# Weighted rows of the second experts added on TensorE at the end of a hybrid attention, HGRN2 and mixture-of-experts step

## What is computed

```python
x = x + concat([att, rec]) @ w_o
h = rmsnorm(x, norm2_g)
for e in range(N_EXPERTS):                      # each row: its two best experts
    y = (silu(h @ w_gate[e]) * (h @ w_up[e])) @ w_down[e]
    out = out + gates[..., e:e + 1] * y
x = x + out
y_prompt, y_sample = rmsnorm(x, final_norm_g)
```

## Time and profile before

| | |
|---|---|
| median of three runs | 523.42 us (521.96 to 525.18) |
| the profiled execution | 524.19 us |
| its span in the trace | 522.4 us |
| PE busy | 471.7 us (90%) |
| DVE (VectorE) busy | 336.5 us (64%) |
| ACT (ScalarE) busy | 232.0 us (44%) |
| POOL (GpSimd) busy | 105.7 us (20%) |
| DMA, mean over the span | 178 GB/s |

### The profile page before, as it was taken

The page is one execution under the profiler, slowest core; times in us unless marked ns, Lnnn a source line. Parts: engine busy times, 40 slices in busy tenths (PEclk is TensorE's granted clock), DMA queues, the critical chain, the costliest instruction groups (busy, mean ns, idle before and its releaser), DMA issues.

```text
span 522.4 us, 7082 instructions
## 1 busy us (share of the span) xinstructions
PE 471.7 (90%) x2493; PEld 371.8 (71%) x2493; DVE 336.5 (64%) x658; ACT 232.0 (44%) x448; POOL 105.7 (20%) x168
## 2 busy tenths in 40 slices
PE   6999899999999999999999887999999999999400
PEld 6879799877996777778877686676766776677100
DVE  4777515586585357766554689697478567765176
ACT  6664711563356447224121335466367356544021
POOL 5148001111000000001000143030322322312143
PEclk9999999999999999999999959899999999999855
DMA  8804404004008500510110878999899999800295
GB/s 306 194 6 163 169 0 162 0 1 162 1 1 218 163 11 4 178 41 0 41 60 3 304 271 344 421 404 373 333 367 377 375 342 358 338 23 27 69 332 189
DMA packets 33101, 93.16 MB, mean 178 GB/s; under 512 B 10248, under 2 KB 13456, under 8 KB 26928
## 3 DMA queue, kind: packets, MB, share of 16 engines
q1 hardware_dynamic: 27728, 82.81, 44.0%
q0 software_dynamic: 5344, 9.97, 5.4%
HBM read 88.38 MB, written 13.89 MB: 196 GB/s over the span
## 4 chain that ended last, share of the span: by engine, by line
PE 77%; DVE 11%; DMA 5%; ACT 4%; issue 1%; SPq 1%; POOL 0%; POOLq 0%; ACTq 0%; DVEq 0%
PE ps L2069 11%; PE ps L1745 7%; PE ps L1747 7%; PE ps L1746 7%; PE ps L2089 6%; PE ps L2091 5%; PE ps L2090 5%; PE ps L1957 3%; PE ps L1959 3%; PE ps L1958 3%; DMA pair<-y_pairs 2%; PE ps L2050 2%; PE ps L1982 1%; PE ps L1900 1%; PE ps L1897 1%
## 5 line engine op out<-in xcount | busy, mean ns | idle before, releaser
L1610 DVE TENSOR_TENSOR gu_lo<-we_gu,gu_hi 128x1024 fp32r<-128x1024 f32 x64 | 74.8, 1219 | 3.0 <-ACT gu_hi L1004 1.5
L1004 ACT ACTIVATE gu_hi<-we_gu 128x1024 fp32r<-128x1024 f32 x64 | 63.2, 1055 | 3.0 <-DMA we_gu<-in_w_up 3.0
L2069 PE MATMUL ps<-we_d,hhT 128*128 128x512 f32 x128 | 56.9, 592 | 0.0
L2089 PE MATMUL ps<-gu_hi,xT_hi 128*128 128x512 f32 x128 | 52.7, 411 | 2.6 <-DVE xT_lo L1604 2.5
L2091 PE MATMUL ps<-gu_hi,xT_lo 128*128 128x512 f32 x128 | 50.9, 397 | 0.0
L2090 PE MATMUL ps<-gu_lo,xT_hi 128*128 128x512 f32 x128 | 50.5, 395 | 0.0
L1745 PE MATMUL ps<-hT_hi,w_hi 128*128 128x288 f32 x160 | 48.5, 303 | 1.7 <-DVE w_lo_q L1103 0.8
L2069 PEld LDWEIGHTS ps<-we_d,hhT 128*128 128x128 f32 x128 | 23.4, 191 | 24.9 <-issue 24.9
L1745 PE MATMUL ps<-w_hi,hT_hi 128*128 128x512 f32 x96 | 39.1, 407 | 0.0
L1746 PE MATMUL ps<-w_lo,hT_hi 128*128 128x512 f32 x96 | 37.5, 391 | 0.0
L1745 PEld LDWEIGHTS ps<-hT_hi,w_hi 128*128 128x128 f32 x160 | 30.1, 188 | 5.0 <-issue 2.6
(11 more groups left out here) (394 smaller groups left out, 1122.3 us busy)
## 6 DMA issues: line engine op xcount, KB each, us to landing
we_gu<-in_w_gate SPq DMA_DIRECT2D x16, 1024.0 KB, 7.7
we_gu<-in_w_up SPq DMA_DIRECT2D x16, 1024.0 KB, 13.0
we_d<-in_w_down SPq DMA_DIRECT2D x16, 1024.0 KB, 12.3
ring<-in_w_in SPq DMA_DIRECT2D x4, 2048.0 KB, 7.7
pair<-y_pairs SPq DMA_DIRECT2D x8, 512.0 KB, 7.7
ring<-in_w_in SPq DMA_DIRECT2D x3, 1024.0 KB, 8.1
x_first<-in_x_p SPq DMA_DIRECT2D x4, 512.0 KB, 9.7
x<-in_x_p SPq DMA_DIRECT2D x4, 512.0 KB, 3.7
```

The lines of the kernel that those rows point to most:

```text
L1004: act.activation(gu_hi[slot % 2][:, :, 2 * q:2 * q + 2, :], we_gu[slot][:, :, 2 * q:2 * q + 2, :], ACT.Copy).then_inc(gu_hi_done, 1)
L1610: dve.tensor_tensor(gu_lo[slot][:, :, 2 * q:2 * q + 2, :], we_gu[slot][:, :, 2 * q:2 * q + 2, :], gu_hi[slot % 2][:, :, 2 * q:2 * q + 2, : ...
L2069: last = pe.matmul(bank(4 + 2 * (slot % 2) + half), hhT[:, slot % 2, f, :], we_d[slot][:, f, 512 * half:512 * half + 512], start=f == 0, s ...
L2089: pe.matmul(bank(0), xT_hi[:, c, :], gu_h[:, :, c, :], start=c == 0, stop=False)
```

## The change

For tiles 1 to 4 the residual and the second experts' rows are added on TensorE. Four diagonal 128x128 matrices with the second gates on their diagonals are made by VectorE at the end of `weights()`, in the memory of a gain that is no longer needed (`ng_bc`). After the last group of blocks TensorE multiplies the identity with x of tiles 1 to 4, each tile into two banks of PSUM, and then, when a tile's second rows have landed, adds the diagonal matrix times these rows in the same banks. VectorE's `weigh_first(t)` adds the first experts' rows, weighted, to what stands in PSUM and writes x. Tile 0 keeps its two instructions. The ten loads are issued in another order, and the finals of tiles 1 to 4 stand behind all of the weighing.

```diff
+        diag = ng_bc[:, :].rearrange("p (t k) -> p t k", t=NT - 1)
...
+        diag_ready, added = sem("diag_ready"), sem("added")
...
-            for t in range(NT):
-                for i in range(2):
+            for t, i in ((1, 1), (0, 0), (2, 1), (0, 1), (3, 1), (1, 0), (4, 1), (2, 0), (3, 0), (4, 0)):
                     cols = slice(i * D, (i + 1) * D)
                     sp.dma_start(pair[0:rows_of(t), t, cols], pairs[tok(t), cols]).then_inc(pair_in[i][t], 16)
...
-                act.wait_ge(sum_ready, 2 * t + 2)
+                act.wait_ge(sum_ready, t + 2)
...
                 dve.tensor_tensor(gates[:, 1, :], gates[:, 0, :], rb[:, :, 4], ALU.mult).then_inc(gates_ready, 1)
+                dve.wait_ge(gates_ready, 1)
+                for t in range(1, NT):
+                    dve.tensor_scalar(diag[:, t - 1, :], ident[:, :], gates[:, 1, t:t + 1], None,
+                                      ALU.mult).then_inc(diag_ready, 1)
...
+            def weigh_first(t):
+
+                r = rows_of(t)
+                dve.wait_ge(added, t)
+                dve.wait_ge(pair_in[0][t], 16)
+                dve.scalar_tensor_tensor(x[0:r, t, :], pair[0:r, t, 0:D], gates[0:r, 0, t:t + 1],
+                                         ps[0:r, 2 * t - 2:2 * t, :].rearrange("p b n -> p (b n)"),
+                                         ALU.mult, ALU.add).then_inc(sum_ready, 1)
...
             weigh(0)
-            weigh(1)
-            for t in range(2, NT):
-                weigh(t)
-                final(t - 2)
-            final(NT - 2)
-            final(NT - 1)
+            weigh_first(1)
+            weigh_first(2)
+            final(0)
+            weigh_first(3)
+            weigh_first(4)
+            for t in range(1, NT):
+                final(t)
...
+            pe.wait_ge(diag_ready, NT - 1)
+            pe.wait_ge(xT_dve, 2 * UNROLL * turns + 2)
+            pe.wait_ge(y_act, UNROLL * turns + 2)
+            pe.wait_ge(y_dve, UNROLL * turns + 2)
+            for t in range(1, NT):
+                r = rows_of(t)
+                for half in range(2):
+                    pe.matmul(ps[0:r, 2 * t - 2 + half, :], ident[0:r, 0:r], x[0:r, t, 512 * half:512 * half + 512],
+                              start=True, stop=False)
+            for t in range(1, NT):
+                r = rows_of(t)
+                pe.wait_ge(pair_in[1][t], 16)
+                for half in range(2):
+                    last = pe.matmul(ps[0:r, 2 * t - 2 + half, :], diag[0:r, t - 1, 0:r],
+                                     pair[0:r, t, D + 512 * half:D + 512 * half + 512], start=False, stop=True)
+                last.then_inc(added, 1)
```

More of the change, by code:

```diff
@@ L1677, in weigh @@
                                              x[0:r, t, :], ALU.mult, ALU.add).then_inc(sum_ready, 1)
-                    dve.wait_ge(sum_ready, 2 * t + i + 1)
+                    dve.wait_ge(sum_ready, i + 1)
+            def weigh_first(t):
[5 more added lines that the diff above has]
+                                         ALU.mult, ALU.add).then_inc(sum_ready, 1)
             def final(t):
```

## The result

The changed kernel takes 526.42 us, the median of 15 runs (524.07 to 527.78), beside 523.42 us for the kernel before (15 runs on the same chip, 520.88 to 525.18). The ratio is 1.0058, 95% interval 1.0040 to 1.0076: slower by 0.6%, within the forecast's "within 1%", but a gain of 0.6 us had been forecast and the time is 3.6 us above the predicted 522.8 and outside the range. The profiled execution took 526.78 us with a span of 525.0, 2.6 us more than before, and the last store lands 3.3 us behind the last final in both.

A forecast was written before the change was run, and what follows sets the result against it. The end behind TensorE's last matmul was taken as bound by loads, then VectorE: of 5.1 us of weighings removed, 0.6 remain, 524.19 to 523.6 profiled; the median, 0.8 lower, is 522.8. Range 521.3 to 525.2.

The forecast's parts named there:

- What bounds the end: Behind TensorE's last matmul: a DMA holds the first 15 us, then VectorE works almost without pause, its last final awaiting GpSimd.
- The landings: Ten loads of experts' rows: 1.43 us per 512 KB, eighth landing at 507.5, between 507.2 and 509.4.
- VectorE behind the eighth landing: From weigh_first 2 at 507.5, steps of 1.20 us and two GpSimd holds bring final 4's end to 518.5.
- Late loads, the rival: Eighth load lands at 509.4 as before: +1.3 us, 524.7; decides from a landing at 508.1; chance 0.17.
- The clock rival: TensorE's clock falls near 491.7 despite identity matmuls, so weigh_first 4 waits for its pair: +2.6 us, 526.0; chance 0.10.
- The clock: TensorE beside the loads: clock stays at 1.00 to about 508, pairs of matmuls done well ahead.
- GpSimd: Small instructions before finals 3 and 4 wait for the running VectorE instruction's end: pauses of 0.4 and 0.7 us.
- PSUM as an input: weigh_first reading PSUM instead of SBUF on VectorE costs 0; the skill's 62 cycles would be 0.2 us for three.
- The matrices: Four diagonal matrices made by VectorE in the first group of experts: 1.1 us, hidden by a later wait of 2.90 us.
- theory C: Theory tested in the follow-up runs: the new order of load addresses is slow in itself, with 128-row loads too.

The follow-up runs named there:

- experiment 4: The changed kernel, but its seventh load fetches 128 rows (tile 3's second experts) instead of tile 4's 64: 524.09 us, ratio 1.0005 to the kernel before.
- experiment 1: The changed kernel with the 64-row load of tile 4's second rows moved from seventh to ninth place: 524.34 us, ratio 1.0012 to the kernel before.
- Experiment 5: The changed kernel with loads tile by tile, tile 4 last, and finals between the weighings: 521.79 us, ratio 0.9956 to the kernel before.
- experiment 9: The kernel before, without TensorE work, with each final t-1 right behind weigh t on VectorE: 523.46 us, ratio 1.0004.
- experiment 6: The changed kernel with loads tile by tile, tile 4 last, and VectorE's list unchanged: 524.03 us, ratio 0.9996 to the kernel before.
- experiment 7: The changed kernel with the load order of experiment 1 and the VectorE order of Experiment 5: 522.51 us, ratio 0.9979 to the kernel before.
- experiment 10: The kernel of Experiment 5 with the identity matmuls of tiles 1 and 2 done twice: 521.39 us, ratio 0.9950 to the kernel before.

## Why the prediction was wrong, step by step

**What bounds the end: right.** A DMA holds it, and then VectorE, with GpSimd ahead of the last two finals.

**The landings: the step that failed, a size.** The prediction set the seventh load at half of 1.43 us for its 256 KB, and so the eighth landing at 507.5 (+13.7), with 509.4 as the latest bound. It landed at 510.7 (+17.1). It was the term of the loads that was mis-sized. By experiment 4 the eighth lands at +14.5 with a full load of 128 rows in the seventh place: so of the 3.4 us, 0.8 are what the fourth run has more than the forecast (0.7 of it the other 256 KB, at the pace of the forecast), and 2.6 are that the 64-row load is dearer than the full one. Priced by experiment 1, where the same load is the seventh and not the eighth, the 64-row load ahead of it costs 17.1 - 13.2 = 3.9 us; I had given it 0.7. The number was to be had: the kernel before has two loads of this kind, and beside them its rate fell from 393 to 164 GB/s. I read that as a matter of the time, 507 us, and of the coming store ("the slump can touch only the last tenths of this load"), and it went with tile 4's loads wherever they stood (+13 in the kernel before and in experiment 1, +10.5 in the changed kernel).

**VectorE behind the eighth landing: right.** Forecast from 507.5 to 518.5, 11.0 us; measured 510.74 to 521.69, 10.95 us, with the pauses of 0.4 and 0.7 us where they were foretold. With the true landing the sum is -0.6 + 3.2 = +2.6 us on the profiled execution, 526.8, and it took 526.78. With the same list on VectorE and full loads up to the ninth place (experiment 4) the last final ends at +25.6, no sooner than before; the forecast's gain of 0.6 us stood on the half load in the seventh place being cheap.

**Late loads, the rival: right in kind.** Its place was right, and the point from which it decides too (508.1, or +14.3: experiment 4, with weigh_first 2 at +14.6, ends its last final at +25.6, 0.3 later than before). Its price of 1.3 us was too small, since it took the eighth landing of before as the worst. That landing had only full loads ahead of it. (The clock rival's 526.0 lies nearer to the measured 526.42; that is chance, since weigh_first never waited for TensorE.)

**The clock: the fall came, its price did not.** The forecast had 1.00 to 508. Its mean was 0.65 between 502 and 503, behind a pause of TensorE of 2.58 us and half a microsecond of work; it was 0.50 from 503 to 505 and 1.00 again from 506 on (0.79 is the mean from 504 to 508). The pair of tile 2 took longer, as the changed kernel's TensorE rows show, and weigh_first 4 ran 3.2 us behind the end of the last pair (509.16 + 1.93 = 511.09):

```profile
489.43 7.25 PE L2137 MATMUL ps<-x,ident 128*128 128x512 f32 x16 [0.88 <-DVE y L1644]
497.22 1.98 PE L2143 MATMUL ps<-pair,ng_bc 128*128 128x512 f32 x4 [0.55 <-DMA pair<-y_pairs]
501.79 5.43 PE L2143 MATMUL ps<-pair,ng_bc 128*128 128x512 f32 x8 [2.58 <-DMA pair<-y_pairs]
509.16 1.93 PE L2143 MATMUL ps<-pair,ng_bc 64*64 64x512 f32 x4 [1.94 <-DMA pair<-y_pairs]
```

Two pairs take 5.43 us instead of twice 1.98; part of that is no loss, since tile 3's rows landed at +11.2, 504.7, and its pair could not start before. A pair takes 1.98 us also at 2.4 GHz, where I had 1.72. The identity matmuls are at 489.43 to 496.68, forecast 489.6 to 496.5. Experiment 5 is where the price fell due.

**GpSimd: right in its sum, too wide in its rule.** I had it wait for the end of any VectorE instruction that runs when it starts. Its rows in the changed kernel:

```profile
513.29 0.19 POOL L632 TENSOR_SCALAR ms<-stats 128x1 f32<-128x1 f32 x1 [2.43 <-ACT pair L1067]
...
515.67 1.18 POOL L632 TENSOR_SCALAR ms<-stats 128x1 f32<-128x1 f32 x1 [1.57 <-ACT pair L1067]
516.94 1.44 POOL L633 TENSOR_TENSOR stats<-ms,neghalf 128x1 f32<-128x1 f32 x1
518.47 1.28 POOL L632 TENSOR_SCALAR ms<-stats 64x1 f32<-64x1 f32 x1
```

Beside weigh_first 3 (513.13), which reads PSUM, the instruction takes 0.19 us; beside finals, which read x and the gain in SBUF, 1.18 and 1.28. Experiments 5 and 9 have the two kinds again. Of the 38 small instructions of GpSimd that begin beside a weigh_first in all the traces, 37 are short (0.19 us for `ms`, up to 0.58 for the power). One disagrees, in experiment 6, begun 0.05 us behind the start of weigh_first 4 (513.86 to 515.13):

```profile
513.91 1.63 POOL L633 TENSOR_TENSOR stats<-ms,neghalf 128x1 f32<-128x1 f32 x1
```

Why, no run tells. The rest is what the Trainium skill states, page "SBUF — State Buffer", section "Who interferes with whom": a VectorE instruction with two inputs in SBUF contends with a GpSimd instruction that reads SBUF, one with at most one does not. The traces agree but for that row. The difference changed nothing in the sum, because four finals stand at the end of the changed kernel's list; in experiment 5 it keeps the finals between the weighings from waiting.

**PSUM as an input: 0, right.** weigh_first takes 1278 ns on average and tile 0's weighings 1285. The 62 cycles more that the page "VectorE: DVE Perf Modes" of the Trainium skill, in its section on the TRN2 errata, gives PSUM sources do not show.

**The matrices: hidden, right.** They took 0.88 us (forecast 1.1), and the wait behind them is still there, as VectorE's timeline shows:

```profile
328.84 0.88 DVE L1540 TENSOR_SCALAR ng_bc<-ident,gates 128x128 f32<-128x128 f32 x4
...
334.93 0.42 DVE L1651 TENSOR_TENSOR hh<-sg,ps 128x256 f32<-128x256 f32 x1 [2.95 <-ACT sg L1050]
```

**Open.** The second to fifth landings of the changed kernel are 0.5 to 1.1 us late, and the third is as late (+7.9 to +8.2, against +7.0 to +7.6) in every run whose first loads go to three different tiles, also without matmuls. It is a second slump, with loads of 128 rows alone: in the two microseconds from +4 on the rate is 238 GB/s in the changed kernel and 242 in experiment 4, against 414 in the kernel before. So something of theory C is left. Why, no run tells. The landings of one and the same kernel also differ by up to 0.8 us between two executions (the eighth of the two profiles of the fifth run: +14.9 and +15.7), and what sets that is open too.

## What to carry to other kernels

Before a transfer is moved forward in a queue, price it by what one like it did in the trace and not by its bytes alone: look for the rate while it was under way, and count the loads on both sides of it. A transfer of few partitions is the first to suspect. Work taken off the engine that follows the loads can be given back by a late load ahead of it and by the order of what stands behind it: here 5.1 us of VectorE won nothing until the 64-row loads stood last and the finals between the weighings (experiments 5 and 7); the loads in VectorE's order alone gave nothing (experiment 6). Then see which engine is late next; here it was TensorE with a fallen clock, and GpSimd held up by VectorE instructions that read SBUF twice.

## What the hardware showed that I had not expected

- One load of 256 KB to 64 partitions (tile 4's rows) in the seventh place delays the load behind it by 2.6 us more than one of 512 KB to 128 partitions (tile 3's), and makes the load issued ahead of it late as well (+13.8 against +11.9). The share of busy DMA engines is 1.03 in both cases and tells nothing of it; the GB/s do (210 and 399).
- TensorE's clock was at 0.50 after it had been idle for 4.07 us behind a full stretch of 7.25 us, and some 3.5 us of matmuls that nobody needs kept it at 1.00 (experiments 5 and 10).
- A GpSimd instruction on one column takes 0.19 us beside a VectorE instruction with one input in PSUM and up to 1.3 us beside one with both in SBUF; one power, of 38 such instructions, broke this, with 1.63 us beside a weighing that reads PSUM.
